# The low halves of split weight blocks: subtracted on GpSimd, or added by an accumulating transfer

## The reference

```
m = silu(c) @ ada_w + ada_b                      # six modulation vectors
h = rmsnorm(x) * (1 + sc1) + sh1
z = h @ w_in                                     # 1024 x 8448
rwkv7 (both directions), neighbourhood attention, retention (both directions)
merged = gates[0]*out_a + gates[1]*out_b + gates[2]*out_c     # each branch through its own projection
x = x + g1 * rmsnorm(merged @ w_out)
h2 = rmsnorm(x) * (1 + sc2) + sh2
u = dwconv3(h2 @ ffn_up); val, gate = split(u)   # 1024 x 5632
x = x + g2 * rmsnorm((gelu(gate) * val) @ ffn_down)           # 2816 x 1024
```

## Time and profile before

| | before |
|---|---|
| median of three runs | 2025.21 us |
| profiled execution, its time | 2030.75 us |
| span from first to last instruction | 2028.6 us |
| mean granted TensorE clock | 0.982 |
| busy: TensorE, VectorE, ScalarE, GpSimd | 94%, 49%, 46%, 47% |
| chain that ended last: PE, DVE, ACT, POOL, DMA | 79%, 9%, 4%, 2%, 2% |
| bytes read from HBM | 223.58 MB |

### The profile page before, as it was taken

How to read it: one execution, slowest core, us unless ns; L and a number is a source line. 1 busy time by engine, 2 the same in 40 slices (tenths; PEclk the granted TensorE clock), 3 DMA queues, 4 the chain that set the end, 5 groups by cost and what they waited for, 6 DMA issues and landing times.

```text
span 2028.6 us, 41739 instructions
## 1 busy us (share of the span) xinstructions
PE 1905.9 (94%) x17940; PEld 1718.9 (85%) x17940; DVE 1001.8 (49%) x1516; ACT 939.8 (46%) x1766; POOL 944.0 (47%) x767
## 2 busy tenths in 40 slices
PE   6899999999999989999988999999999998999997
PEld 2887878797899879999947878787879997899996
DVE  2574747475611255552057657475745133555502
ACT  4554645454533454443345555364554334544432
POOL 1434426170666626666416153342516664466663
PEclk9999999999999989999989999999999999999998
DMA  7314232232443314434453141413224432244442
GB/s 291 101 50 143 64 117 94 89 115 86 135 124 122 120 63 124 124 122 127 123 204 124 50 140 55 136 65 125 87 88 156 125 125 83 94 125 125 125 125 73
DMA packets 65414, 231.52 MB, mean 114 GB/s; under 512 B 7376, under 2 KB 11856, under 8 KB 64592
## 3 DMA queue, kind: packets, MB, share of 16 engines
q1 hardware_dynamic: 59040, 215.21, 33.3%
q10 hardware_dynamic: 6192, 13.66, 1.9%
HBM read 223.58 MB, written 5.26 MB: 113 GB/s over the span
## 4 chain that ended last, share of the span: by engine, by line
PE 79%; DVE 9%; ACT 4%; issue 3%; POOL 2%; DMA 2%; ACTq 1%; SPq 0%; DVEq 0%; POOLq 0%
PE psz L471 57%; PE psw L471 20%; DVE work L1360 3%; ACT work L954 3%; DMA ring<-in_w 2%; POOL ringlo L1735 1%; DVE work L1369 1%; PE psz L479 1%; PE psw L479 1%; ACT whi L954 1%; DVE rstd L1369 1%; DVE part L1360 1%; DVE work L1363 1%; POOL work L1771 1%; DVE work L1366 0%
## 5 line engine op out<-in xcount | busy, mean ns | idle before, releaser
L1735 POOL TENSOR_TENSOR ringlo<-ring,whi 128x512 fp32r<-128x512 f32 x608 | 811.1, 1357 | 756.7 <-ACT whi L954 756.7
L471 PE MATMUL psz<-hhi,whi 128*128 128x386 f32 x1696 | 587.1, 346 | 23.2 <-POOL ringlo L1735 14.5
L471 PE MATMUL psz<-hlo,whi 128*128 128x386 f32 x1696 | 577.6, 341 | 0.0
L471 PE MATMUL psz<-hhi,ringlo 128*128 128x386 f32 x1696 | 576.4, 340 | 0.0
L954 ACT ACTIVATE whi<-ring 128x1024 fp32r<-128x1024 f32 x304 | 320.2, 1053 | 133.4 <-PE psz L471 125.1
L471 PE MATMUL psw<-work 64*64 64x64 f32 (+4 forms) x9024 | 348.8, 232 | 17.6 <-issue 9.1
L471 PEld LDWEIGHTS psw<-work 64*64 64x64 f32 (+2 forms) x9024 | 294.5, 137 | 73.1 <-issue 55.6
L471 PEld LDWEIGHTS psz<-hhi,whi 128*128 128x128 f32 x1696 | 321.0, 189 | 36.1 <-issue 18.9
L471 PE MATMUL psz<-part,whi 128*128 128x386 f32 x1344 | 346.6, 339 | 3.2 <-DVE work L1360 1.5
L471 PEld LDWEIGHTS psz<-hlo,whi 128*128 128x128 f32 x1696 | 322.9, 190 | 2.1
L471 PEld LDWEIGHTS psz<-hhi,ringlo 128*128 128x128 f32 x1696 | 321.0, 189 | 0.0
(11 more groups left out here) (107 smaller groups left out, 1725.2 us busy)
## 6 DMA issues: line engine op xcount, KB each, us to landing
ring<-in_w SPq DMA_DIRECT2D x400, 512.0 KB, 3.5
pk<-in_pk ACTq DMA_DIRECT2D x8, 832.0 KB, 4.4
const<-in_const SPq DMA_DIRECT2D x1, 1795.0 KB, 10.0
work<-in_x SPq DMA_DIRECT2D x1, 1544.0 KB, 6.8
work<-in_x ACTq DMA_DIRECT2D x1, 1544.0 KB, 6.5
out_x<-work ACTq DMA_DIRECT2D x1, 1544.0 KB, 5.5
work<-out_x ACTq DMA_DIRECT2D x1, 1544.0 KB, 9.8
out_x<-work SPq DMA_DIRECT2D x4, 386.0 KB, 2.3
```

Source lines behind the costliest of these rows:

```text
L471: ins = nc.tensor.matmul(out, a, b, start=start, stop=stop, skip_group_check=True)
L1735: L.do(G.tensor_tensor(out, a, b, op), S[sig] if sig else None)
```

## The change

The low half is no longer subtracted on GpSimd. ScalarE's `split` makes a second pass: behind the rounding copy it reads the block once more and writes it, negated and rounded to fp32r (so the negated high half), into the ring slot, over the raw block, and only this raises `w_hi`. Behind that GpSimd issues a transfer that fetches the same block from HBM again and adds it to what is in the slot, so that the slot holds the block minus its high half. Each slot has a semaphore of its own for this, `w_low`, which counts 16 for each transfer; TensorE waits for it through `low_in(j)` in all places where it waited for `w_lo`.

```diff
-            sq_used=..., w_hi=len(SPLIT), w_lo=2 * len(SPLIT), w_used=48, x_upd=KT,
+            sq_used=..., w_hi=len(SPLIT), w_used=48, x_upd=KT,
...
+        w_low = [sem(f"w_low{i}") for i in range(RING)]
...
+            SLOT_LOWS = [sum(b % RING == s for b in SPLIT) for s in range(RING)]
+
+            def low_in(j):
+
+                s = SPLIT[j] % RING
+                n = sum(b % RING == s for b in SPLIT[:j + 1])
+                return w_low[s].h, 16 * (SLOT_LOWS[s] * turn[0] + n)
...
                     def dense(zi, j, src=hsp, wait=None, between=None):
                         out = opened(zi)
-                        pe.wait_ge(*after("w_lo", 2 * j + 2))
+                        pe.wait_ge(*low_in(j))
...
                         act.wait_ge(*block_in(b))
                         if j >= 3 or layer:
                             act.wait_ge(*read_up(j - 3))
-                        run(high(j), ring[:, b % RING * 1024:(b % RING + 1) * 1024], sig="w_hi")
+                        raw = ring[:, b % RING * 1024:(b % RING + 1) * 1024]
+                        run(high(j), raw)
+                        run(wlo[b % RING], raw, ACT.Copy, "w_hi", scale=-1.0)
...
                         pool.wait_ge(*after("w_hi", j + 1))
                         a = SPLIT[j] % RING
-                        for i in range(2):
-                            part_ = slice(512 * i, 512 * i + 512)
-                            tt(wlo[a][:, part_], ring[:, a * 1024 + 512 * i:a * 1024 + 512 * i + 512],
-                               high(j)[:, part_].bitcast(F32), ALU.subtract, sig="w_lo")
+                        pool.dma_start(wlo[a], wstream[layer, SPLIT[j]],
+                                       accum_op=ALU.add).then_inc(w_low[a].h, 16)
```

More of the change, by code:

```diff
@@ L111 @@
             mod_ready=2, mrg_ready=KT, row_done=4, row_ready=4 + 3 * PAIRS, rt_root=4, sq_ready=4 * KT,
-            sq_used=2 * (KT - 1), sum_used=2 * (KT - 2), ss_done=4, w_hi=len(SPLIT), w_lo=2 * len(SPLIT), w_used=48, x_upd=KT,
+            sq_used=2 * (KT - 1), sum_used=2 * (KT - 2), ss_done=4, w_hi=len(SPLIT), w_used=48, x_upd=KT,
             prm_in=16, pk_in=16 * PAIRS, out_k=32 * PAIRS, out_st=32 * PAIRS, x_ld=16)
@@ L331, in trunk @@
             sctx_ready sd_ready sig_ready silu_c sq_ready sq_used sum_used ss_done st0_ready st_done
-            til_ready tv_ready u_done u_ready v_step vt_done vt_ready w_hi w_lo w_used wm_done x_ld x_st wm_ready
+            til_ready tv_ready u_done u_ready v_step vt_done vt_ready w_hi w_used wm_done x_ld x_st wm_ready
             x_init x_in cc_in const_in cleared x_ready x_upd xi_ready xt_done y_copied y_done yc_ready yroot_ready yv_done
@@ L519, in dense3 @@
                                     opened(zi + i)
-                                    pe.wait_ge(*after("w_lo", 2 * (j + i) + 2))
+                                    pe.wait_ge(*low_in(j + i))
                                 three(z(zi + i), j + i, n, src[n], n == 0, n == KT - 1, "z_done" if n == KT - 1 else None)
@@ L525, in dense2 @@
                         out = [opened(zi), opened(zi + 1)]
-                        pe.wait_ge(*after("w_lo", 2 * j + 4))
+                        pe.wait_ge(*low_in(j))
+                        pe.wait_ge(*low_in(j + 1))
                         for k in range(KT):
```

## The result

The changed kernel takes 2327.91 us (median of 4 runs, 2323.1 to 2344.34), the kernel before 2023.13 us beside it. The ratio is 1.151, 95% interval 1.147 to 1.156. The forecast was 2145 us in a range of 2050 to 2330: the direction was right and the size was not; the rise is 305 us where 120 were forecast. The time lies at the upper end of the range, which was drawn to reach the rivals, and not by the sum. The nearest number is that of the rival "the DMA engines fill up", 2315.

A forecast was written before the change was run, and what follows sets the result against it. TensorE, 94% busy, was taken as the bound, with GpSimd mostly waiting. Pair turns 63, dense runs inside 6, start of up 9.5, output 8, steady stages 41, less 8 relief: +120 us, forecast 2145, range 2050 to 2330.

The forecast's parts named there:

- the DMA engines fill up: Rival, dense blocks: a two-stream transfer costs twice a plain one's engine time, 5.12 us a block, total 2315; chance 0.22 (shared).
- The second pass: ScalarE, each split block: a second 1.05 us copy, ScalarE's own part 2.11 us, 320 us in all, 62% busy.
- middle of a turn: Pair turns: low half 3.14 us becomes 6.3, second copy adds 1.05, tensor_scalar falls by 0.5; sum +3.7 a turn.
- start of up: First split after the three interleaved blocks: its block is ready at 747.75 instead of 743.00, +4.75, twice, +9.5 us.
- L: Time from GpSimd's issue to the landed low half: 2.5 to 2.9 us before, taken as 6.3 after the change.
- The interpolation over plain loads: Part of the landing estimate: reading 1024 KB, between plain loads of 832 and 1544 KB, gives 5.0 us.
- The formula: Dense block: the larger of 4.27 us and a third of 4.27, ScalarE's work, 0.15 handover and issue-to-landing time.
- Steady dense stages, +41: Landing at 6.3 us slows up by 22, merge by 12, output projection by 5 and down by 2 us.
- Its sign, a share near 1.0: Test for the full-engines rival: up and down projections take 320 us or more with DMA share near 1.0.
- an estimate of 4.4 us: Landing by the skill's formula, 2.0 us plus bytes at 436 GB/s, bytes read twice; sum then about +33, not +120.
- The relief of VectorE: Start of layer 1's merge: tensor_tensors without GpSimd's subtractions beside them fall to about 0.56 us, giving back about 8 us.
- the change doesn't relieve GpSimd: Rival: an issue takes 2.7 us like the subtractions, GpSimd stays 47% busy, total 2290; chance 0.22 shared with full engines.

## Why the prediction was wrong

**The bound and the place: right.** TensorE waits where a half is late, and nearly all of GpSimd's 811 us were off the path. The second pass on ScalarE, and the handoffs, are where the trace of before had put them: middle of a turn 5.72 us for 3.14, start of up +5.8 for +4.75.

**L: no constant, and too low in the steady stages.** I took 6.3 us. The landing line of the `ringlo` tile in the trace (all 304 transfers):

```profile
DMA to landing us min/median/max: 5.1/7.0/12.8
```

At the two places of the earlier trace rows the 5.72 and 5.24 us are under the forecast; in the steady stages the chain shows 7 to 9 us. So L is 5.1 us at best and longer where the engines are busy, up to 12.8, and the ring loads themselves went from 3.5 to 5.2. The interpolation over plain loads gave 5.0 us, near the 5.1; the 1.3 us for an issue on top were too many. It left out that the transfer holds the engines twice as long (3.06 us to 1.52) in a stage where they were 40% busy already. The forecast had this in the rival, at a chance of 0.22, and nothing of it in the sum. The formula with L = 7.2 gives 4.82 us for a block of up; 5.06 was measured. The rest, 0.24 us a block, is probably gaps that don't close again and the clock behind them, which no term of mine held.

**The steady stages: the step that failed.** The forecast took a block as the larger of 4.27 us and the loop at L = 6.3, with no term for the time that both transfers of a block need of the DMA engines. "Steady dense stages, +41" became +144 (merge 43, up with down 101), with 24 more in the output projection where 13 were forecast, and this carries most of the miss. In its place the runs show 5.06 us a block in up with down: the engines need some 4.58, and the landing of 7 to 9 us closes the loop above that (six buffers for three took 31 of the 49 us away). The rival's figure of 1.20 x 4.27 = 5.12 us a block is near the measured 5.06 in part by luck. Its sign, a share near 1.0, is met in the merge (0.93) but not in up with down (0.87), where the loop stands above the engines. The Trainium skill (Collectives: The Full Stack, Why ReduceScatter is half of AllGather) has a reduction at half of a copy's rate because of the two source reads. The queue rows agree roughly: 3.06 us is 2.0 times the ring load's 1.52 beside it, and 1.7 times the 1.81 of the plain transfer that GpSimd issues. The Trainium skill's formula for a transfer's fixed and variable part (DMA: Bandwidth & Descriptors, Anatomy of one DMA), from which the prediction made an estimate of 4.4 us with both reads counted, is below the fastest of 304 landings, 5.1 us. For the plain transfer from GpSimd the same formula gives an estimate of 3.2 us, against 3.6 measured at best and 4.4 in the median.

**The second pass: undersized.** Counted at 2.1 us a turn and 4.2 at four starts, 21 us; 38 measured on the kernel before.

**The relief of VectorE: it came, and where 8 us were forecast it was worth nothing.** The tensor_tensors at the start of layer 1's merge (timeline of VectorE) against the earlier trace rows:

```profile
1719.92 0.56 DVE L1372 TENSOR_TENSOR mix<-work 128x386 f32<-128x386 f32 x1
1720.40 1.97 DVE L1372 TENSOR_TENSOR part<-mix,part 128x386 fp32r<-128x386 f32 x4
1723.32 1.97 DVE L1372 TENSOR_TENSOR part<-mix,part 128x386 fp32r<-128x386 f32 x4 [0.95 <-ACT part L964]
1729.48 1.97 DVE L1372 TENSOR_TENSOR part<-mix,part 128x386 fp32r<-128x386 f32 x4 [4.19 <-ACT part L964]
```

They take 0.5 us each, but come in three parts with waits of 0.95 and 4.19 us for the high parts that ScalarE makes behind its two passes. Those waits are not what the stretch lost. VectorE is off the chain there now, and the accumulating transfer of 11.90 us at 1719.98 holds TensorE until 1732.03, so the stretch lost 10 us instead of gaining 8. The forecast let the next thing on the path be free. In the middle of a turn the relief did count, by 0.8 us (0.38 for 1.16), where 0.5 was forecast.

**GpSimd's issue** takes 0.88 us where I assumed 1.3 for the issue as a part of L, so "the change doesn't relieve GpSimd" is refuted, although its time, 2290, is near the measured one too.

**Open:** what the lower clock costs by itself, and how much of the merge's 43 us behind its first six gates is the engines' and how much the loop's; the buffers were deepened in up and down alone. TensorE's busy time rose by 93 us with the same matmuls, so the clock's part of the 305 us may be anything up to about that.

## What to carry to other kernels

An accumulating transfer cost the DMA engines here 1.7 to 2.0 times a plain one, so before a pass is given to it, add its time per block to the share of the stage in which it runs, and not to the mean of the kernel: 0.40 plus twice 0.40 is past full, whatever the mean over the span says. A half that was made in 2.7 us on an idle engine and comes back as a transfer of 5 to 9 us eats the slack of the loop (3.9 us here); measure it first. More buffers gave back 76 of the 305 us and no more. And an engine that mostly waits is a poor place to look for time: at 64 KB a block GpSimd had all of its relief, and the kernel was still 2% slower, with twice the copies on ScalarE.

## What was not expected of the hardware

- An accumulating transfer costs about twice a plain one: 3.06 us of all 16 engines per 512 KB against 1.52 for the ring load, and 1.81 for the plain transfer issued by GpSimd. Adding 256 KB costs about what moving 512 KB does (1.69 us).
- GpSimd's issue of a transfer takes 0.88 us with the addition, whether 64, 256 or 512 KB follow, and 0.545 us without it (512 KB).
- The landing of an accumulating transfer: 2.7 us for 64 KB, 4.1 for 256, 7.0 for 512 (medians), with 5.1 the fastest of the last. Beside a 1544 KB load, at a share of 0.98, one took 11.90 us.
- VectorE's tensor_tensors of 386 columns took 0.50 to 0.56 us beside GpSimd's issues, against 1.02 to 1.56 us beside its subtractions. So an issue did not hold them up.
